# Hybrid attention layer on one Trainium2 core: ScalarE's and VectorE's order inside a softmax step is changed from "both tiles, stage by stage" to "tile by tile"

## The reference, cut to what matters

```python
# branch A, per head; branch B has a sink column too
s_nb  = einsum(q, k_near) * HEAD_DIM ** -0.5 + bias      # 256 near keys
s_ctx = einsum(q, k_cached) * HEAD_DIM ** -0.5           # 512 cached keys
p = softmax(concat([s_nb, s_ctx]))
o = einsum(p_near, v_near) + einsum(p_ctx, v_cached)
```

## Time and profile before

| | |
|---|---|
| median of 3 executions | 1152.59 us (1151.6 to 1155.74) |
| the profiled execution | 1153.9 us, its span 1152.1 us |
| PE busy | 1087.0 us (94%) |
| PEld busy | 963.9 us (84%) |
| DVE busy | 778.6 us (68%) |
| ACT busy | 623.7 us (54%) |
| POOL busy | 96.3 us (8%) |
| mean granted TensorE clock | 0.975 |

### The profile page before, as it was taken

How to read it: one execution, slowest core, us unless ns; L and a number is a source line. 1 busy time by engine, 2 the same in 40 slices (tenths; PEclk the granted TensorE clock), 3 DMA queues, 4 the chain that set the end, 5 groups by cost and what they waited for, 6 DMA issues and landing times.

```text
span 1152.1 us, 18389 instructions
## 1 busy us (share of the span) xinstructions
PE 1087.0 (94%) x6459; PEld 963.9 (84%) x6459; DVE 778.6 (68%) x1539; ACT 623.7 (54%) x1126; POOL 96.3 (8%) x111
## 2 busy tenths in 40 slices
PE   7999899999999999998899899799988699999997
PEld 1899789989989998997788789689777599898896
DVE  6869668767757776774875886787668576445343
ACT  5832337636655763663574665567476574443342
POOL 0000200000000000000000000000000063443430
PEclk9999999999999999999999899899989899999999
DMA  9825618855992983798487398388386895542630
GB/s 360 316 76 158 189 62 161 187 170 105 194 225 48 185 189 114 160 183 220 85 174 167 67 183 189 96 176 166 85 190 151 208 313 176 175 164 91 218 128 37
DMA packets 318975, 188.34 MB, mean 163 GB/s; under 512 B 256166, under 2 KB 297766, under 8 KB 318892
## 3 DMA queue, kind: packets, MB, share of 16 engines
q1 hardware_dynamic: 305068, 165.31, 58.7%
q10 hardware_dynamic: 13824, 21.96, 6.0%
HBM read 94.27 MB, written 32.12 MB: 110 GB/s over the span
## 4 chain that ended last, share of the span: by engine, by line
PE 56%; DVE 14%; ACT 10%; DMA 9%; SPq 5%; issue 5%; DVEq 0%; POOL 0%; ACTq 0%
PE d_ps_pairs L94 11%; PE s_ps_pairs L94 11%; PE y_ps L2076 10%; PE b_ps L94 9%; PE v_ps L94 4%; PE o_ps_pairs L1215 4%; ACT pr L1329 4%; DVE pl L1654 3%; ACT ph L1349 3%; SPq L1095 3%; DMA xl<-pl 3%; DVE mn L1577 3%; PE s_ps_pairs L1162 2%; PE s_ps_pairs L1163 2%; DMA xh<-ph 2%
## 5 line engine op out<-in xcount | busy, mean ns | idle before, releaser
L94 PE MATMUL d_ps_pairs<-h,wt 128*128 128x384 f32 (+4 forms) x1848 | 352.6, 346 | 0.0
L94 PEld LDWEIGHTS d_ps_pairs<-h,wt 128*128 128x128 f32 x1848 | 319.7, 189 | 14.4 <-issue 0.6
L94 PE MATMUL s_ps_pairs<-h,wt 128*128 128x512 f32 (+1 forms) x864 | 175.5, 362 | 0.0
L1329 ACT ACTIVATE pr<-s_ps_pairs,mx 128x896 f32<-128x896 f32 (+1 forms) x128 | 124.8, 978 | 75.9 <-DVE mx L1599 75.8
L94 PEld LDWEIGHTS s_ps_pairs<-h,wt 128*128 128x128 f32 x864 | 145.1, 194 | 22.7
L1654 DVE SCALAR_TENSOR_TENSOR pl<-pr,rden,ph 128x896 f16<-128x896 f32 (+1 forms) x128 | 137.5, 1116 | 29.9 <-ACT ph L1349 16.3
L1349 ACT ACTIVATE ph<-pr,rden 128x896 f16<-128x896 f32 (+1 forms) x128 | 124.1, 1009 | 1.1 <-issue 0.8
L2076 PE MATMUL y_ps<-wo,mg 128*128 128x512 f32 (+1 forms) x504 | 113.2, 385 | 0.0
L2076 PEld LDWEIGHTS y_ps<-wo,mg 128*128 128x128 f32 x504 | 91.3, 188 | 20.6
L2030 POOL TENSOR_TENSOR tp<-tp 128x256 f32<-128x256 f32 x40 | 31.2, 781 | 832.6 <-DVE tp L2155 831.9
L94 PE MATMUL b_ps<-og,wb 128*128 128x256 f32 x720 | 87.6, 282 | 0.7 <-DVE tp L2155 0.7
(11 more groups left out here) (236 smaller groups left out, 1615.1 us busy)
## 6 DMA issues: line engine op xcount, KB each, us to landing
wraw<-in_w_gate SPq DMA_DIRECT2D x24, 512.0 KB, 4.0
gt<-gates_d SPq DMA_DIRECT2D x40, 256.0 KB, 4.4
wada<-in_w_ada SPq DMA_DIRECT2D x12, 512.0 KB, 7.1
gates_d<-craw ACTq DMA_DIRECT2D x30, 192.0 KB, 3.3
oz<-gates_d SPq DMA_DIRECT2D x20, 256.0 KB, 4.1
oz<-o_d SPq DMA_DIRECT2D x20, 256.0 KB, 3.9
x_f<-in_x SPq DMA_DIRECT2D x10, 512.0 KB, 6.4
y<-y_f SPq DMA_DIRECT2D x9, 512.0 KB, 2.7
```

The source lines that it names most:

```text
L94: mm = eng.matmul(out, lhs(a, k), rhs(b, k), start=(k == 0 and i == 0), stop=(k == n_k - 1 and i == 2))
L1329: act.activation(probs_run(s, t), scores_run(s, t), ACT.Exp, bias=mx[:, t:t + 1], scale=-1.0, accum_out=den[:, t:t + 1]).then_inc(exp_done, 1)
```

## The change

ACT and DVE go through steps 1 to 8 tile by tile. On ACT the order "exponential 0, exponential 1, upper 0, upper 1" becomes "exponential 0, upper 0, exponential 1, upper 1". On DVE "minima, add_halves, scale 0, tile_lows, scale 1, lower 0, lower 1" becomes "minima, scale 0, add_halves, tile_lows, lower 0, scale 1, lower 1". No instruction is added or removed; PE's and SP's programs, all waits of single instructions and step 0 stay as they are.

```diff
-            def exps(s):
-                for t in range(2):
+            def exps(s, tiles=(0, 1)):
+                for t in tiles:
...
-            def upper(s):
+            def upper(s, tiles=(0, 1)):
 
                 n = pb * STEPS + s
-                for t in range(2):
+                for t in tiles:
...
                 if s > 0:
-                    exps(s)
-                upper(s)
+                    for t in range(2):
+                        exps(s, (t,))
+                        upper(s, (t,))
+                else:
+                    upper(s)
                 gate(s)
...
-            def lower(s):
+            def lower(s, tiles=(0, 1)):
 
                 n = pb * STEPS + s
-                for t in range(2):
+                for t in tiles:
...
                 if s > 0:
                     minima(s)
+                if s > 0:
+                    scales(s, 0)
                 if s >= 2:
                     add_halves(s - 2)
                 if s > 0:
-                    scales(s, 0)
                     tile_lows(s - 1)
+                    lower(s, (0,))
                     scales(s, 1)
-                lower(s)
+                    lower(s, (1,))
+                else:
+                    lower(s)
```

## The result

The changed kernel takes 1222.5 us (median of 4, 1220.8 to 1224.0) against 1153.6 us for the kernel before, run beside it: a ratio of 1.0605, 95% interval 1.0574 to 1.0636, so 69 us more. The forecast was 1215 with a range of 1188 to 1234, and 0.94 on slower. No instruction was added, so the busy times of DVE and ACT hardly move (778.6 to 785.0 us, 623.7 to 634.5 us); the span grows from 1152.1 to 1220.8 us.

What follows compares the result with a forecast made beforehand. B was taken as bound by a DVE-ACT loop, A by PE. A 22 + B 37 + DMA 4 = 63 us on the profiled 1153.9 gives 1217, less 1.3 for the median: 1215 us, range 1188 to 1234.

Steps and rivals of the forecast that it cites:

- The bound: Branch B bound by a DVE-ACT-DVE loop with 7.85 us beats; A's 7.32 us loop hides under PE's 7.7.
- What comes onto the chain: Plain step: one `lower` leaves (-1.07), two scales and two hand-overs come on; B 9.04 us, A 8.37 us.
- Weight tiles: Steps 2, 4, 6 (and 8 in A): `tile_lows` and `add_halves` delay `lower` 0, adding 0.24 us (B), 0.21 (A).
- the second step of each pair: Step 2 of a pair, treated like any weight-tile step: `add_halves` 0.41 us (A), 0.57 (B); beats 8.58 and 9.28.
- B's first beat: First step of B's pairs: both tiles edge tiles, scores late and at low clock; 8.7 us against 7.61 now.
- A's pairs: Seven beat intervals of a pair in branch A sum to 58.1 us, now 52.6: 5.5 more a pair.
- Given back between pairs: Between pairs of A, the next projection starts sooner after the last beat, returning 0.6 us; nothing after A's last pair.
- DMA landings, +4 us: xl transposes lose some 1 us of room before `lower` 0; waits -12 to +14 us, taken as +4.
- (a) PE hides A: Rival: PE hides A's loop if it gains 0.4 us or less; only B grows: 1190 us; chance 0.10.
- (b) PE bounds all: Rival: PE is the bound everywhere, so ACT and DVE may wait at no cost: 1153 us; chance 0.03.
- (c) Earlier transposes: Rival, faster: tile 0's `ph` done earlier, its transpose starts earlier, cutting `lower`'s DMA waits; down to 1140.6 us; chance 0.03.
- (d) The clock: Rival: PE's pauses in B steps lower the clock; beat 9.5, 0.5 more on 28 steps, 1230 us; chance 0.10.

Runs made afterwards that it cites:

- experiment 6: Kernel before, with `lower` of tile 1 moved behind the next step's minima (steps 1 to 7): 1150.7 us, 0.9981 of before.
- experiment 11: Kernel before, with `lower` of tile 1 moved behind the next step's minima and a second buffer for pl: 1150.3 us, 0.9987 of before.
- experiment 1: Changed kernel with only ACT's new order, DVE's step loop as before: 1205.6 us, 1.046 of before.
- experiment 2: Changed kernel with only DVE's new order, ACT's step loop as before: 1231.2 us, 1.068 of before.
- experiment 3: Kernel before, with a 128x256 memset on DVE between tile 0's sum and reciprocal in each full step: 1155.9 us, 1.0032 of before.
- experiment 4: Changed kernel, with a 128x256 memset on DVE between tile 0's sum and reciprocal in each full step: 1238.1 us, 1.0755 of before.
- experiment 7: Changed kernel, with `add_halves`, `tile_lows` and `low_half` moved into idle holes and SP's weight-tile load behind the ph transposes: 1263.4 us, 1.096 of before.
- experiment 8: Changed kernel with the idle holes filled, SP's weight-tile load behind the ph transposes, and a second buffer for pl: 1221.9 us, 1.0606 of before.
- experiment 9: Changed kernel with only a second buffer for pl, used in turn, order of work unchanged: 1220.6 us, 1.0586 of before.
- experiment 10: Kernel before with a second buffer for pl, used in turn: 1150.0 us, 0.9978 of before.
- experiment 5: Kernel before with the change in branch A alone, B in its old order: 1180.1 us, 1.0246 of before.

## Why the prediction was right, point by point

- **The bound.** The loop from DVE to ACT and back in B was right. A's 0.4 us of room under PE holds for its late steps; in the second and third the loop of 7.32 us sets the beat itself. In B the loop was nearer to PE's bound than I had it: experiments 6 and 11 took a `lower` of 1.07 us off it and gained 1.6 to 1.8 us a pair on average.
- **What comes onto the chain.** Right for a plain step. Beats without a wait for a landing lie within 0.01 to 0.02 us of the sum (9.03 to 9.05 and 8.37 to 8.38; 7.91 with an edge tile). Experiments 1 and 2 show that each engine's order costs what its own sum says, and 3 and 4 that tile 0's scale came onto the chain.
- **Weight tiles.** 8.57 in A (8.58 forecast), 9.40 in B (9.28): from the reciprocal's start to `lower` 0 it takes 0.08 + 0.59 (`add_halves`, two instructions) + 1.15 = 1.82 us. The forecast had 1.70, a slip: its own terms 0.08, 0.57 and 1.12 make 1.77.
- **The term that was mis-sized: the second step of each pair.** I took `add_halves` at 0.41 and 0.57 us in every step. In step 2 it handles the prompt, which is twice as wide (0.85 us for its two instructions), and it falls together with a weight tile. The beat was 9.15 in A and 9.71 to 9.83 in B, for 8.58 and 9.28: 4 us in all. From B's second pair of the changed kernel:

```profile
700.37 0.16 DVE L1638 RECIPROCAL rden<-den 128x1 f32<-128x1 f32 x1
700.48 0.85 DVE L1687 TENSOR_TENSOR ost<-o_ps_pairs,otmp 64x256 f32<-64x256 f32 x2
701.36 1.23 DVE L1669 TENSOR_TENSOR wt<-wraw,wt 128x1024 fp32r<-128x1024 f32 x1
702.50 1.15 DVE L1657 SCALAR_TENSOR_TENSOR pl<-pr,rden,ph 128x896 f16<-128x896 f32 x1
```

B's first beat was 9.08, not 8.7: the scores start 5.69 us behind the beat (693.10 less 687.41), take 3.16 at the low clock level, and the reduction follows 0.23 later. With the 9.40, that is most of why B's pairs grew by 38.8 and not 35.6. Experiments 7 and 8 show the cause: with `add_halves` in a hole and `tile_lows` in another, step 2 falls to 8.47 and 9.18 (9.53 in the last pair).
- **A's pairs** grew by 30.1 us, not by 22 (4 x 5.5). Step 2 is 2.3 of the 8 us and the landings 4.1 (experiment 9). The other 1.6 come from the value before: the forecast took 52.6 us for every pair, from the second, and the mean of the four is 52.2.
- **Given back between pairs.** 0.3 us a pair in A (44.1 to 43.8), not 0.6. Behind the second pair the projection did start 0.63 us sooner after the last beat (5.58 for 6.21), but its matmuls took 5.73 us for 5.46; why was not looked into. Behind the last pair of A nothing came back, as forecast: the stretch grew by 0.9 us.
- **DMA landings, +4 us.** Neither borne out nor refuted. The waits did not grow (12.0 us), and the totals of experiments 9 and 10 give the buffer nearly the same worth before and after. But A's pairs say 4.1 us after and nothing before, since waits that PE's work had hidden now lie on the chain, and B's say 1.6 us the other way.
- **What was luck.** A's 22 us came out 8 too low, and the 4 us set aside for landings in both branches made up for half of that.
- **(a) PE hides A**: refuted by experiment 5. **(b) PE bounds all**: refuted by the 69 us. PE has the highest busy share, by matmuls and by weight loads (94% and 84%). The Trainium skill, Perfetto Trace Analysis, Identifying the Most-Contended Engine, takes the engine with the highest occupancy for the one to optimize first; here that would have pointed to PE. A chain over two engines that are busy 54% and 68% set the pace; such a chain shows in the beat, not in a busy share.
- **(c) Earlier transposes**: the high half of tile 0 is done earlier (710.28 + 1.04 is 5.1 us behind its beat), and no wait that sets the pace ended with it.
- **(d) The clock.** Part of it occurs. In B the granted clock went from 0.96 to 0.94. At the end of the third and the start of the fourth step of B's second pair PE, which had idled 2.29 us before its scores, was granted the low level (1.2 GHz) for part of this window of the changed kernel:

```profile
714.00:718.00 4.00, 4.00 (x21) 2.90 (x21) 3.67 (x7) 2.02 (x5) 0.00 (x0) 0.60 0.73 154
```

ACT's `low_half`, ahead of the exponential, waited for PE there, and the exponential came 0.4 us late:

```profile
717.47 0.38 ACT L1396 ACTIVATE otmp<-o_ps_pairs 64x256 f32<-64x256 f32 x1 [1.48 <-PE o_ps_pairs L1215]
717.88 1.01 ACT L1329 ACTIVATE pr<-s_ps_pairs,mx 128x896 f32<-128x896 f32 x1
```

That beat took 9.79 us instead of 9.40. The third step of B's first pair has the same, with its scores at the low level, and is 0.47 us longer than its like (9.51 for 9.04). Two more such stretches lie in the last pair (928 to 936 and 952 to 957 us), where no beat is more than 0.1 us over its like. So it is 1 us in all, not the 0.5 us a step of my rival. That the new pauses caused it is not shown: after the same pause of 2.3 us in the third step of the other two pairs (816.98 and 916.83 us) full clock was granted, and the kernel before has one such stretch too (866 to 872 us, 0.72). The Trainium skill, TensorE: Matmul & The Clock Gate, A second HAM failure mode: psum-queue depth-cycling, tells of a kernel whose clock oscillated with short idle times between its groups of matmuls; this trace agrees so far as two of four like pauses were followed by the low level.

## What to carry to other kernels

Two tiles that go through a chain over two engines together hide each other's hand-overs; going tile by tile can put every small instruction between the engines (a sum, a reciprocal) onto the chain, as it did here, and where that chain closes on itself from step to step it costs this in every step, however idle the engines look. Write down one step as a zigzag with its starts, before and after the edit, and look at each kind of step, the widest above all: here the plain steps came out to 0.02 us and the error sat in the odd ones and in waits for transfers. When an order is changed in one queue, look at what the neighbours in that queue wait for: one load put right ahead of two transposes, and issued later, came with 60 us of waits.

## What the runs showed that was not expected

- With the 512 KB load of a weight tile between the transposes of ph and of pl, issued in half of the steps or fewer, `lower` waited 60.2 us for landings in 28 places between 160 and 1000 us, and the kernel took 1263.4 us; with a second buffer for the transposes' source and the same order it took 1221.9.
- The stretch up to the first beat, whose code is the same in all, took between 169.3 and 173.4 us in these profiles; a term of 2 us read off a pair of single profiles is within that.
